# Which engine issues the rope's half-swaps: SyncE or ScalarE

## The chip, the cores and the metric

One core of a Trainium2 chip. The time is that of one execution of the whole program on the device, in microseconds (us): 3450.16 us, the median of 3 runs (3445.27 to 3460.52).

## The reference, cut to what matters

A sequence of 512 tokens of width 1024 goes through two blocks. The first has two layers (SwiGLU, stick-breaking attention or a linear recurrence, SwiGLU). The second has two *hybrid* layers, and the change lies in these alone:

```python
proj = h @ w_in                       # a_q, a_k, ..., b_q, ..., i_q, i_k, ..., c_q, c_k, ...
ya = moba_attention(apply_rope(heads(a_q, 6)), apply_rope(heads(a_k, 6)), heads(a_v, 6))
yb = dsa_attention(apply_rope(heads(b_q, 6)), rope1(b_k), b_v, apply_rope(heads(i_q, 4)), rope1(i_k), i_w)
yc = dilated_mixture(apply_rope(heads(c_q, 12)), apply_rope(heads(c_k, 12)), heads(c_v, 12))

def apply_rope(x, cos, sin):          # heads of 64 columns
    x1, x2 = x[..., :32], x[..., 32:]
    return concatenate([x1 * c - x2 * s, x1 * s + x2 * c])
```

Every rope needs, beside each half of 32 columns of a head, the other half. `dsa_attention` first scores all keys with the small index heads (i_q, i_k) and keeps the best; its selection precedes the heads B.

## The kernel before, in words

Activations lie transposed: columns of a projection on the partitions, the 512 tokens along the free axis. A projection is made in *panels* of 256 columns. For each panel SyncE loads 1 MB of weights into one of four `raw` buffers (L2523); ScalarE casts them to a high part (`w_high`, L1172); VectorE subtracts to get a low part (`w_low`, L1670); TensorE (PE) multiplies high by high, high by low and low by high into a pair of PSUM banks (L579). Each engine has its own program, written out in the order in which it shall work, and waits on semaphores for named steps. `take(key)` in an engine's program means: do the loads, casts or subtractions up to some panels ahead of this one. SyncE loads up to three panels ahead, ScalarE and VectorE one ahead.

A hybrid stage (`h0`, `h1`) has, before the heads, the panels i_q, a_v, i_k, a_q (two), a_k, a_v, a_g. Behind the first a_q panel stand the four index scores on PE (L914), whose sums VectorE makes and then searches for the largest (L2104, L2106). Then come 24 heads (6 A, 6 B, 12 C in three groups of four), pipelined: in step `i` PE turns the weights of head `i-2`, makes one panel that `L.fills` names for this step, makes the scores of head `i+1`, and the values of head `i-2`. ScalarE's order in step `i` is: copy of the turned weights (L1498), the exponentials of head `i-1` (L1504), `fill_rest`, `fill` (casts, then the copy out of PSUM), and `finish` of head `i-2` (L1243, or L1559 and L1566 for C). VectorE's is: row maximum of head `i` (L2154), weights of head `i-1` (L2167, L2170), the rope of the panel before, `w_low`, `finish`.

The rope of a panel, 13 of them in a stage:

1. ScalarE copies the product from PSUM to `rope_x` (`rope_copy`, L1441; step `roped_in`). It first waits until the previous rope has left `rope_x` (`x_free`).
2. The halves are swapped from `rope_x` into `rope_y` by DMA: four transfers of 32 partitions, 128 KB each (two of 64 KB for i_k). In the kernel before, SyncE does this (`swap`, L2579 to L2588): it waits for the copy and until the previous rope has left `rope_y` (`y_free`: its last `roped`), and issues the transfers. They stand in SyncE's program between the `take`s that load weights.
3. When they have landed (`swapped`), GpSimd multiplies the first half-panel by cos (L2410), VectorE the second (L2062), both by sin (L2063), and VectorE adds (L2066; step `roped`).

There is one `rope_x` and one `rope_y`. The ropes come in the order i_q, i_k, a_q 0, a_q 256, a_k 128, b_q 0, b_q 256, and for each C group c_q and c_k; from b_q on they are the fills of steps 0, 1, 5, 6, 9, 12, 15 and 16. Two more transfers on SyncE, `copy_half` (L2593), double the roped ik and bk.

Of the kernel before, what the change touches and what calls it, by code (L numbers as in the profile page):

```python
# [55 lines left out]
def build(nc, t, out):  # L56
# [6 lines left out]
    HD = 64  # L63
# [11 lines left out]
    with ExitStack() as ctx:  # L75
# [3 lines left out]
        def sem(name):  # L79
            return ctx.enter_context(nc.semaphore(name))  # L80
# [26 lines left out]
        with nc.sbuf_tensor("before_parts", [P, 12 * S], F32), nc.sbuf_tensor("sb_parts", [P, 4, TRI], F32R) as sb_parts:  # L107
# [15 lines left out]
        s_in, s_tab, s_swap, s_out, s_gate_w, s_dup = (sem(n) for n in (  # L123
            "x_loaded", "tables_loaded", "swapped", "stored", "gate_w_loaded", "copied_half"))
# [4 lines left out]
        def at(*step):  # L129

            return steps.get(step, (None, 0)) if counting[0] else steps[step]

        def fence(q, name):

            for engine in ENGINES:
                q.wait_ge(*at("past", name, engine))
# [152 lines left out]
        for m, (kind, i) in enumerate(entries):  # L289
# [4 lines left out]
            r = min(allowed, key=lambda r: -1 if newest_in[r] is None else newest_in[r])  # L294
# [865 lines left out]
        def scalar(q):  # L1160
            e = q.engine
# [15 lines left out]
            def taken_product(key):  # L1177
                q.wait_ge(*at("product", *key))
                b = base_of.get(key, 0)
                return psum[:, b:b + 2, :]  # L1180
# [251 lines left out]
            def hybrid(layer):  # L1432
                stage = f"h{layer}"
                L = hybrid_views(layer)

                def rope_copy(name, c0):

                    for step in L.x_free(name, c0):
                        q.wait_ge(*at(*step))
                    parts, n = L.parts(name, c0), len(L.dests[name, c0])  # L1440
                    e.copy(L.rope_x[0:parts[0], 0:n, :], taken_product((stage, name, c0))[0:parts[0], 0:n, :]).then_inc(  # L1441
                        *q.up(s_taken, "roped_in", stage, name, c0))

                def gate_sigmoid(name, c0):
                    dst = L.gates[name, c0]
                    n = dst.shape[1]
                    e.activation(dst, taken_product((stage, name, c0))[:, 0:n, :], ACT.Sigmoid).then_inc(*q.up(s_taken, "gate_sigmoid", stage, name, c0))
                    e.preload_act_table_set("natural_log_exp_and_others")
# [8 lines left out]
                q.mark("past", (stage, "area"), "ACT")  # L1457
                fence(q, (stage, "area"))
                rope_copy("i_q", 0)
                key = (stage, "a_v", 0)  # L1460
                q.wait_ge(*at("product", *key))
                b = base_of.get(key, 0)
                e.copy(L.av[:, :, 0:256], flat[:, b * 512:(b + 2) * 512].rearrange("p (t c) -> p t c", c=PANEL)).then_inc(*q.up(s_taken, "av", stage, 0))
                take((stage, "i_k", 0))
                rope_copy("i_k", 0)
                e.mul(L.SS[0][64:68, 0:S], psum[64:68, base_of.get((stage, "i_k", 0), 0), :], 1.0 / 16.0).then_inc(*q.up(s_taken, "iw_scaled", stage))
                take((stage, "a_q", 0))
                rope_copy("a_q", 0)
                q.wait_ge(*at("iw_turned", stage))
                e.copy(L.iw, psum[:, 5, 0:16].rearrange("p (n h) -> p n h", n=NT)).then_inc(*q.up(s_taken, "iw", stage))  # L1470
# [16 lines left out]
                b = base_of.get(("av_turned", stage), 0)  # L1487
# [128 lines left out]
            for j in range(KD):  # L1616
                q.wait_ge(*at("x_turned", j))
                b = base_of.get(("x_turned", j // 2 * 2), 0)
# [16 lines left out]
            rglru()  # L1635
            ffn("f3")
            hybrid(0)
            hybrid(1)
            spread("end2", 1)
            for n in range(NT):  # L1640
                q.wait_ge(*at("out_turned", n))
                b = base_of.get(("out", n), 0)
# [865 lines left out]
        def sync(q):  # L2508
            e = q.engine
# [23 lines left out]
            def take(key):  # L2533
                split_to(ahead_of(number[key]))

            def first_products(stage):
                split_to(number[stage, *FIRST[stage][0]] + 1)

            def project_back(stage, row0, last=True):
                if last:  # L2540
                    split_to(beyond_back(stage, row0, NC + 1))
                    return
                for c in range(NC):
                    take((stage, "back", row0, c))
# [30 lines left out]
            def hybrid(layer):  # L2575
                stage = f"h{layer}"
                L = hybrid_views(layer)

                def swap(name, c0):  # L2579

                    parts, n = L.parts(name, c0), len(L.dests[name, c0])
                    q.wait_ge(*at("roped_in", stage, name, c0))
                    for step in L.y_free(name, c0):
                        q.wait_ge(*at(*step))
                    for r in range(0, parts[0], HD):
                        m = sum(1 for p in parts[:n] if p > r)
                        for a, b in ((r, r + 32), (r + 32, r)):
                            e.dma_start(L.rope_y[a:a + 32, 0:m, :], L.rope_x[b:b + 32, 0:m, :]).then_inc(*q.up(s_swap, "swapped", stage, name, c0, by=16))  # L2588

                def copy_half(which, dst, *after):  # L2590
                    for step in after:
                        q.wait_ge(*at(*step))
                    e.dma_start(dst[HD:P, :, :], dst[0:HD, :, :]).then_inc(*q.up(s_dup, "copied_half", stage, which, by=16))  # L2593

                first_products(stage)
                fence(q, (stage, "area"))
                swap("i_q", 0)
                take((stage, "i_k", 0))
                swap("i_k", 0)
                take((stage, "a_q", 0))  # L2600
                copy_half("ik", L.ik, ("roped", stage, "i_k", 0, 0))
                swap("a_q", 0)
                take((stage, "a_q", 256))
                swap("a_q", 256)
                take((stage, "a_k", 128))
                swap("a_k", 128)
                take((stage, "a_v", 256))
                take((stage, "a_g", 128))
                for i in range(len(L.heads) + 2):
                    if i - 1 in L.fills and L.fills[i - 1][1:] == ("b_q", 256):  # L2610
                        copy_half("bk", L.bk, ("roped", stage, "b_q", 256, 0), ("roped", stage, "b_q", 256, 1))
                    if i in L.fills:
                        what, name, c0 = L.fills[i]
                        take((stage, name, c0))
                        if what == "rope":
                            swap(name, c0)
                take((stage, "m_g", 2 * D))
                for jj in range(KD // 2):
                    if jj:
                        for b in range(3):  # L2620
                            take((stage, "m_g", b * D + jj * PANEL))
                    take((stage, "branches", jj))
                project_back(stage, 0)


            for g, names in enumerate(groups):
                r = 0
# [20 lines left out]
            rglru()  # L2648
            ffn("f3")
            hybrid(0)  # L2650
            hybrid(1)
            for n in range(NT):
                q.wait_ge(*at("out_rows", n))
# [66 lines left out]
```

## Time and profile before

| of the profiled execution | |
|---|---|
| its own time | 3461.18 us |
| its span | 3459.5 us |
| PE busy | 3248.6 us, 94% |
| VectorE (DVE) busy | 1778.1 us, 51% |
| ScalarE (ACT) busy | 1171.5 us, 34% |
| GpSimd (POOL) busy | 165.8 us, 5% |
| mean granted clock of TensorE | 0.959 |
| chain that ended last | PE 81%, DVE 10%, ACT 5% |
| SyncE's swap transfers | 92 of 128 KB and 8 of 64 KB |

Engines work beside each other, so the busy times don't add up. The chain that ended last is followed back from the last instruction, at each step to what released it; it says which engine's work set the end. A row of the timeline has a start, a duration, engine, line and operation, and in square brackets how long the engine stood idle before it and what released it. DMA-issuing instructions aren't counted as busy; they stand on the issuing engine's queue, SPq for SyncE.

### The profile page before, as it was taken

How to read it: one execution, taken by the hardware profiler on the slowest of the kernel's cores; microseconds unless marked ns; L12 is line 12 of the kernel's file. 1: busy time of each engine (PE TensorE's matmuls, PEld its weight loads, DVE VectorE, ACT ScalarE, POOL GpSimd, SP SyncE). 2: the span in 40 equal slices, each digit the busy share in tenths (PEclk: the TensorE clock that was granted, in tenths of full speed). 3: DMA queues.
4: the chain of work that ended last, by engine and by line, in shares of the span. 5: the costliest groups of instructions: out<-in, count | busy, mean ns of one | idle time of the engine just before them, and what ended most of it. 6: DMA issues, size and time to landing. Idle time of an engine off the chain costs nothing.

```text
span 3459.5 us, 38825 instructions
## 1 busy us (share of the span) xinstructions
PE 3248.6 (94%) x16388; PEld 2685.2 (78%) x16388; DVE 1778.1 (51%) x2510; ACT 1171.5 (34%) x1523; POOL 165.8 (5%) x228
## 2 busy tenths in 40 slices
PE   3999998999999999999999998989989998999998
PEld 3887886788888888887888887656768876667687
DVE  5455543245555543357633335876543468655434
ACT  3212244543122322237432233233432323335322
POOL 0000011110000000002100000000000010000000
PEclk7999999999999999999999998999989998889898
DMA  4455521114555342231322223221212232212131
GB/s 178 158 195 170 172 84 49 49 62 158 195 177 176 123 157 97 92 111 54 101 98 98 98 74 92 78 67 57 74 50 96 77 113 67 60 50 74 61 98 49
DMA packets 286551, 353.72 MB, mean 102 GB/s; under 512 B 9458, under 2 KB 263210, under 8 KB 286378
## 3 DMA queue, kind: packets, MB, share of 16 engines
q1 hardware_dynamic: 286378, 351.23, 31.4%
q8 instruction: 130, 2.13, 0.3%
q14 instruction: 43, 0.35, 0.0%
HBM read 336.00 MB, written 2.10 MB: 98 GB/s over the span
## 4 chain that ended last, share of the span: by engine, by line
PE 81%; DVE 10%; ACT 5%; issue 1%; DMA 1%; POOL 1%; SPq 0%; DVEq 0%; ACTq 0%; POOLq 0%
PE psum L579 56%; PE psum L700 6%; PE psum L1104 3%; PE psum L658 2%; PE psum L600 2%; PE psum L973 2%; PE psum L1011 2%; DVE w_low L1670 1%; PE psum L776 1%; PE psum L989 1%; DVE psum L1798 1%; PE psum L545 1%; DVE h_low L1810 1%; DVE area L2106 1%; PE psum L654 1%
## 5 line engine op out<-in xcount | busy, mean ns | idle before, releaser
L579 PE MATMUL psum<-h_high,w_high 128*128 128x512 f32 (+1 forms) x2496 | 993.0, 398 | 51.7 <-DVE w_low L1670 22.0
L579 PE MATMUL psum<-h_low,w_high 128*128 128x512 f32 (+1 forms) x2496 | 984.3, 394 | 0.0
L579 PE MATMUL psum<-h_high,w_low 128*128 128x512 f32 (+1 forms) x2496 | 983.0, 394 | 0.0
L1670 DVE TENSOR_TENSOR w_low<-raw,w_high 128x2048 fp32r<-128x2048 f32 (+2 forms) x246 | 546.2, 2228 | 312.0 <-ACT w_high L1172 311.8
L1172 ACT CAST w_high<-raw 128x2048 fp32r<-128x2048 f32 (+3 forms) x254 | 464.2, 1840 | 546.5 <-DMA raw<-in_ffn_w_gu 253.2
L579 PEld LDWEIGHTS psum<-h_high,w_high 128*128 128x128 f32 (+1 forms) x2496 | 475.4, 190 | 163.1 <-issue 35.8
L579 PEld LDWEIGHTS psum<-h_high,w_low 128*128 128x128 f32 (+1 forms) x2496 | 475.2, 190 | 101.7
L579 PEld LDWEIGHTS psum<-h_low,w_high 128*128 128x128 f32 (+1 forms) x2496 | 475.9, 191 | 99.3 <-issue 1.0
L579 PE MATMUL psum<-y_high,w_high 128*128 128x512 f32 x592 | 233.8, 395 | 11.2 <-DVE w_low L1670 8.6
L1914 DVE TENSOR_TENSOR area<-area,psum 128x512 f32<-128x512 f32 x88 | 60.2, 684 | 342.1 <-PE psum L579 333.8
L579 PE MATMUL psum<-y_high,w_low 128*128 128x512 f32 x592 | 231.9, 392 | 0.0
L579 PE MATMUL psum<-y_low,w_high 128*128 128x512 f32 x592 | 231.8, 391 | 0.0
L1243 ACT CAST y_high<-area 128x512 fp32r<-128x512 f32 x102 | 62.7, 620 | 440.4 <-DVE area L1914 399.0
L1687 DVE SCALAR_TENSOR_TENSOR mod_acc<-raw,vec,mod_acc 128x1024 f32<-128x1024 f32 x126 | 161.9, 1285 | 72.6 <-DMA raw<-in_mod_w 66.8
L1842 DVE SCALAR_TENSOR_TENSOR xT<-psum,gain_out,xT 128x512 f32<-128x512 f32 (+1 forms) x156 | 90.8, 623 | 197.4 <-PE psum L579 158.0
L658 PE MATMUL psum<-h_high,w_high 128*128 128x256 f32 x448 | 134.7, 301 | 14.0 <-DVE w_low L1670 10.7
L579 PEld LDWEIGHTS psum<-y_high,w_high 128*128 128x128 f32 x592 | 111.9, 189 | 36.7 <-issue 10.5
L700 PE MATMUL psum<-y_high,w_high 128*128 128x256 f32 x480 | 139.1, 290 | 1.3 <-DVE w_low L1670 1.1
L700 PE MATMUL psum<-y_high,w_low 128*128 128x256 f32 x480 | 137.2, 286 | 0.0
L700 PE MATMUL psum<-y_low,w_high 128*128 128x256 f32 x480 | 137.2, 286 | 0.0
L658 PE MATMUL psum<-h_low,w_high 128*128 128x256 f32 x448 | 130.2, 291 | 0.0
L579 PEld LDWEIGHTS psum<-y_low,w_high 128*128 128x128 f32 x592 | 112.1, 189 | 23.3 <-issue 0.2
(279 smaller groups left out, 4419.2 us busy)
## 6 DMA issues: line engine op xcount, KB each, us to landing
raw<-in_ffn_w_gu SPq DMA_DIRECT2D x88, 1024.0 KB, 6.3
raw<-in_mod_w SPq DMA_DIRECT2D x72, 1024.0 KB, 5.1
raw<-in_w_in SPq DMA_DIRECT2D x64, 1024.0 KB, 5.2
raw<-in_ffn_w_down SPq DMA_DIRECT2D x32, 1024.0 KB, 7.5
raw<-in_ffn_w_down SPq DMA_DIRECT2D x16, 768.0 KB, 4.8
raw<-in_sb_w_qkv SPq DMA_DIRECT2D x12, 1024.0 KB, 5.1
area<-area SPq DMA_DIRECT2D x92, 128.0 KB, 2.4
raw<-in_lru_w_in SPq DMA_DIRECT2D x10, 1024.0 KB, 5.3
```

The lines of the kernel that those rows point to most:

```text
L579: mm = e.matmul(psum[0:width, base + m, :], wv[a][:, at_k, c0:c0 + width], X[b][:, k, :], start=(at_k == 0 and (a, b) == (0, 0)), stop=(at ...
L600: mm = e.matmul(flat[:, o:o + n], X[b][:, k, tt * P:(tt + 1) * P], wv[a][:, k, :], start=(k == 0 and (a, b) == (0, 0)), stop=(k == KD - 1 ...
L658: mm = e.matmul(psum[:, base + m, HALF[h]], wv[a][:, k, m * P:(m + 1) * P], H[b][:, k, HALF[h]], start=first, stop=last)
L700: mm = e.matmul(psum[:, bank, m * S // 2:(m + 1) * S // 2], wv[a][:, at_k, m * P:(m + 1) * P], X[b][:, k, HALF[h]], start=(at_k == 0 and ( ...
L973: m = e.matmul(flat[:, ROW_AT[n]:ROW_AT[n] + P * (n + 1)], L.q_of(kind, ti)[r0:r0 + HD, n * P:(n + 1) * P], L.k_of(kind, h)[:, 0:P * (n + ...
L1011: m = e.matmul(psum[r0:r0 + HD, OUT, kt * P:S], L.v_of(kind, h, kt), L.PT[:, COL_AT[kt]:COL_AT[kt] + S - P * kt], start=kt == 0, stop=kt = ...
L1104: mm = e.matmul(psum[:, base + m, :], wv[x][:, k, m * P:(m + 1) * P], Y[y][:, k, :], start=(k == k0 and (x, y) == (0, 0)), stop=(k == k1 - ...
L1172: e.copy(w_high[x % NW][:, :n], raw[raw_at[m]][:, :n]).then_inc(*q.up(s_high, "w_high", x))
L1243: e.copy(Y[0][:, k, :], src).then_inc(*q.up(s_act, "y_high", stage, j))
L1670: e.tensor_tensor(w_low[raw_at[m]][:, :n], raw[raw_at[m]][:, :n], w_high[x % NW][:, :n].bitcast(F32), ALU.subtract).then_inc(*q.up(s_low, ...
L1687: g = e.scalar_tensor_tensor(mod_acc[:, :], w, c, mod_acc[:, :], ALU.mult, ALU.add)
L1842: return e.scalar_tensor_tensor(dst, src, gain_out[:, j:j + 1], dst, ALU.mult, ALU.add)
```

## The change

The swaps move from SyncE's program into ScalarE's, behind the copy in `rope_copy`. ScalarE waits for the previous rope to leave `rope_y`, then for its own copy, and issues the same two or four transfers; it goes on with its own program behind them. The transfers, their semaphore and all that waits for them stay. SyncE's program keeps the loads and `copy_half`, in the same order.

```diff
@@ rope_copy (ScalarE) @@
                     e.copy(L.rope_x[0:parts[0], 0:n, :], taken_product((stage, name, c0))[0:parts[0], 0:n, :]).then_inc(
                         *q.up(s_taken, "roped_in", stage, name, c0))
+                    for step in L.y_free(name, c0):
+                        q.wait_ge(*at(*step))
+                    q.wait_ge(*at("roped_in", stage, name, c0))
+                    for r in range(0, parts[0], HD):
+                        m = sum(1 for p in parts[:n] if p > r)
+                        for a, b in ((r, r + 32), (r + 32, r)):
+                            e.dma_start(L.rope_y[a:a + 32, 0:m, :], L.rope_x[b:b + 32, 0:m, :]).then_inc(*q.up(s_swap, "swapped", stage, name, c0, by=16))
@@ hybrid (SyncE) @@
-                def swap(name, c0):
-
-                    parts, n = L.parts(name, c0), len(L.dests[name, c0])
-                    q.wait_ge(*at("roped_in", stage, name, c0))
-                    for step in L.y_free(name, c0):
-                        q.wait_ge(*at(*step))
-                    for r in range(0, parts[0], HD):
-                        m = sum(1 for p in parts[:n] if p > r)
-                        for a, b in ((r, r + 32), (r + 32, r)):
-                            e.dma_start(L.rope_y[a:a + 32, 0:m, :], L.rope_x[b:b + 32, 0:m, :]).then_inc(*q.up(s_swap, "swapped", stage, name, c0, by=16))
...
-                swap("i_q", 0)
                 take((stage, "i_k", 0))
-                swap("i_k", 0)
                 take((stage, "a_q", 0))
                 copy_half("ik", L.ik, ("roped", stage, "i_k", 0, 0))
-                swap("a_q", 0)
                 take((stage, "a_q", 256))
-                swap("a_q", 256)
                 take((stage, "a_k", 128))
-                swap("a_k", 128)
...
                     if i in L.fills:
                         what, name, c0 = L.fills[i]
                         take((stage, name, c0))
-                        if what == "rope":
-                            swap(name, c0)
```

## Rows read from the trace of the kernel before

**Rows 1.** Line L2588: count, duration min/median/max in ns; last row its landings.

```profile
L2588 SPq DMA_DIRECT2D area<-area x100: 507/591/672, 2130.0 to 3138.6; - x100
...
DMA to landing us min/median/max: 2.0/2.4/4.3
```

**Rows 2.** Waits of SyncE's queue, whole span: us in total, times, longest.

```profile
SPq L2588 <- ACT area L1441: 262.7, 20, 26.1
```

**Rows 3.** Line L1172 (casts), 2120 to 2545 us: count, durations; idle before it.

```profile
L1172 ACT CAST w_high<-raw x22: 1055/1898/1912, 2123.2 to 2522.8; 128x2048 fp32r<-128x2048 f32 x21, 128x1024 fp32r<-128x1024 f32 x1
...
  PE psum L658: 1.8, 1
```

**Rows 4.** Timeline of SyncE's queue, stage h0: start us, duration us, issues.

```profile
2132.60 1.34 SPq L2523 DMA_DIRECT2D raw<-in_w_in  x2
2139.11 1.15 SPq L2588 DMA_DIRECT2D area<-area  x2
...
2173.26 2.41 SPq L2588 DMA_DIRECT2D area<-area  x4
...
2245.25 2.41 SPq L2588 DMA_DIRECT2D area<-area  x4
...
2410.14 2.64 SPq L2588 DMA_DIRECT2D area<-area  x4
...
2463.47 2.41 SPq L2588 DMA_DIRECT2D area<-area  x4
```

**Rows 5.** Timeline of VectorE, stage h0.

```profile
2138.33 0.69 DVE L2066 TENSOR_TENSOR y_plain<-y_plain,area 128x512 f32<-128x512 f32 x1
...
2177.47 0.69 DVE L2063 TENSOR_TENSOR area<-area,rope_s 128x512 f32<-128x512 f32 x1 [3.60 <-DMA area<-area]
...
2466.08 0.69 DVE L2154 SCALAR_TENSOR_TENSOR area<-psum,inv 128x512 f32<-128x512 f32 x1 [2.33 <-PE psum L989]
```

**Rows 6.** Chain that ended last, 2128 to 2150 us: start us, us, what.

```profile
2138.47 0.59 ACT area L1466
...
2139.09 1.92 ACT w_high L1172
...
2141.03 2.29 DVE w_low L1670
2143.32 1.70 DVE area L2063
...
2148.10 2.27 PE psum L914 x9
```

**Rows 7.** Timeline of GpSimd at i_k, stage h0.

```profile
2143.10 1.36 POOL L2410 TENSOR_TENSOR y_plain<-area,rope_c 64x512 f32<-64x512 f32 x1 [6.80 <-DMA area<-area]
```

**Rows 8.** Landings of L2588 at 2137 to 2145 us (i_k), at 2845 to 2855 us (a_k).

```profile
DMA to landing us min/median/max: 2.3/2.8/3.3
...
DMA to landing us min/median/max: 2.3/2.4/4.3
```

**Rows 9.** Timeline of ScalarE behind three of its copies, stage h0.

```profile
2247.72 1.01 ACT L1498 COPY area<-psum 128x1024 f32<-128x1024 f32 x1 [2.50 <-PE psum L989]
...
2414.32 1.02 ACT L1498 COPY area<-psum 128x1024 f32<-128x1024 f32 x1 [4.21 <-PE psum L989]
...
2463.34 0.21 ACT L1559 ACTIVATE mod_acc<-mod_acc 128x4 f32<-128x4 f32 x1
```

**Rows 10.** Waits of PE, 2120 to 2545 us: us in total, times, longest.

```profile
PE psum L973 <- DVE y_plain L2073: 5.9, 1, 5.9
...
PE psum L579 <- ACT area L1540: 3.2, 1, 3.2
...
PE psum L914 <- DMA y_plain<-y_plain: 2.4, 1, 2.4
```

**Rows 11.** Chain that ended last: the first two products among the heads of h0.

```profile
2217.87 12.75 PE psum L579 x48
...
2232.97 11.12 PE psum L579 x48
```

## The prediction

> **What bounds the kernel now.** I read the page first. TensorE is busy for 94% of the span and the chain that ended last is 81% PE, so an edit is worth only what it does to PE's waits. The table by line then finds the thing that changes: 100 swap transfers, 50 in each of the two hybrid stages, a median of 0.591 us each for the issue and 2.4 us from issue to landing, all on SyncE's queue [rows 1]. Next come the waits, asked from both ends. What did the swaps keep SyncE from doing? It stood 262.7 us at the head of swap groups waiting for ScalarE's copy [rows 2], with weight loads queued behind. Did a load then come late? The weight casts of the first hybrid stage show one idle stretch, 1.8 us, and its releaser is PE, not a DMA [rows 3]; the second stage answers the same. So SyncE has no time to give back. Last I followed the chain and the timelines around each of the 13 groups of a stage, asking of each: what does ScalarE do in the 2.4 us behind its copy, and who waits for that?
>
> **The change part by part.** The sum is made against the profiled execution, 3461.2 us (span 3459.5); the median of the runs shown is 3450.2, and I carry the difference over to it.
>
> *Taken from SyncE.* 100 × 0.59 = 59 us of issuing and the waits ahead of it. Worth nothing, by the casts that wait for no load [rows 3].
>
> *Given to ScalarE.* Per group one wait for its own copy, one for the previous rope, and four issues (two for i_k). No row shows an issue on ScalarE. The nearest is the same transfer on SyncE: four take 2.41 us, two take 1.15 [rows 4], and I take that, 0.6 us each. Below lies nothing at all (a sequencer that hands the work on and runs ahead); above I set 1.2 us, twice SyncE's median [rows 1]. 0.6 is the only measured price of this very transfer, and both ends are kept as rivals. A wait for its own semaphore I cost at under 0.1 us.
>
> *i_k: on the chain.* Its swaps must wait until the rope of i_q is done, 2138.33 + 0.69 = 2139.02 [rows 5]. Today SyncE does that waiting, and ScalarE goes on with L1466 at 2138.47 and the next weight cast at 2139.09 [rows 6]. Afterwards ScalarE waits itself: swaps from 2139.1 to 2140.3, L1466 to 2140.9, the cast 1.8 us later than now. Everything behind it hangs on that cast in the chain of waits: VectorE's w_low at 2141.03, the rope's multiply L2063, the copy of half of ik by DMA, and PE's index scores at 2148.10, which wait 2.4 us for that copy [rows 6, 10]. A little comes back. L2063 takes 1.70 us here [rows 6] against 0.69 where it runs alone [rows 5], because GpSimd's multiply runs beside it from 2143.10 to 2144.46 [rows 7]; when VectorE comes later, GpSimd is partly done. Between 0 and 1.0 back, I take 0.6: **+1.2 us**.
>
> *i_q and a_q 256: the swaps meet a load.* Today SyncE issues the next loads only after the swaps, at 2132.60 [rows 4]. Freed, it issues them when their buffer is released, about when ScalarE starts its copy, so each group of swaps travels beside 1 MB or 2 MB of weights. VectorE sits 3.60 us waiting for the swaps of a_q 256 [rows 5], and the rope of i_q starts the i_k chain above, so these two landings count. A swap of i_k that now travels beside two loads landed in 3.3 us, and the longest of all took 4.3 [rows 8], against 2.4. From 0 to 1.9 each; I take 0.4, since the group's last swap starts 1.8 us behind its first, when the load is mostly through: **+0.8 us** for the two.
>
> *b_q 256: just covered.* The issues would end at 2245.25 + 2.41 = 2247.66 [rows 4], and ScalarE's next work, L1498, waits for PE until 2247.72 [rows 9]. Behind it stands L1540, for which PE waits 3.2 us [rows 10]: there is no reserve left, and every 0.1 us that an issue costs above 0.6 is 0.4 us of PE. **+0.1 us.**
>
> *c_k 512: the last one.* ScalarE's issues run from 2463.47 to 2465.88, and L1559 (0.21 us, at 2463.34 today) comes behind them, to 2466.1 [rows 4, 9]. VectorE's finish of head 14 waits for L1559, and behind that in VectorE's order stands the row maximum L2154, today at 2466.08 [rows 5], on which PE's next scores wait. **+0.3 us.**
>
> *The other nine cost nothing*, each by a named cover. At c_q 0, c_k 0, c_q 256 and c_k 256 ScalarE's next instruction waits for PE or VectorE until after the issues would end; the tightest is c_k 256, 2410.14 + 2.64 = 2412.8 against 2414.32 [rows 4, 9]. At a_k, b_q 0 and c_q 512 a cast or exponentials come up to 2.4 us later, and a product of 48 matmuls, 11.12 us [rows 11], lies before PE asks for their results. At i_q the copy of a_v moves behind the issues, and its banks are wanted much later. At a_q 0 a small copy (L1470) waits; PE wants it only at the second index head, which the i_k term has itself pushed back. If these covers go, the price is what an issue costs above 0.6, times four.
>
> A longer gap of PE ahead of the index scores could lower the clock behind it. The first product after the 5.9 us gap at the heads' start took 12.75 us against 11.12 for the next of its kind [rows 10, 11]; the gap here grows only from 2.4 to about 4, so 0 to 1.6 us a stage, in the range and not in the sum.
>
> Sum per stage 1.2 + 0.8 + 0.1 + 0.3 = 2.4 us, twice: **+4.8 us**, 3466.0 for such an execution and **3455 us** on the median.
>
> **The rivals.**
> *ScalarE hardly pays (3452).* If an issue costs it nothing, i_k still waits for the rope (cast 0.6 us later, half of it recovered) and the collisions stay: 0.3 + 0.8 = 1.1 a stage, +2.2. For it: nothing but that SyncE's number need not be ScalarE's. Against: SyncE's four issues stand back to back, 2.41 us, as long as a landing [rows 1, 4]. The Trainium skill's page "DMA: Bandwidth & Descriptors", section "Issuing engines are not separate DMA queues", says that issuing from several engines saves only the sequencer's time to start a DMA and calls that usually small beside the DMA; by that rule this rival holds. The rows here disagree on the size.
>
> *The swaps are slowed (3463).* Every landing on the chain goes from 2.4 to 4.3 us [rows 8]: i_q and a_q 256 cost 1.9 each, and at c_k 512 GpSimd's rope comes 1.9 later, of which about 1.0 reaches VectorE. 1.2 + 3.8 + 0.1 + 1.3 = 6.4 a stage, +12.8. For it: the loads now always start beside the swaps. Against: today's median of 2.4 lies near the least landing, 2.0 [rows 1], and a queue of its own takes a swap from behind the load. The same page, section "Queues, rings and completion order", has each DMA engine take turns between queues by packet, so a swap beside a load would get a share at once; that would keep this term small, and no row of one queue can show it.
>
> *An issue costs ScalarE 1.2 us (3470, slower).* Then i_k: 2139.02 + 2.4 + 0.59 − 2139.09 = 2.9; a_q 0: L1470 behind 4.8 us of issues makes the second index head about 1.4 late; b_q 256: 2245.25 + 4.8 − 2247.72 = 2.3, straight into PE's wait for L1540; c_k 512: 2463.47 + 4.8 + 0.2 − 2466.08 = 2.4; collisions 0.8. Together 9.8 a stage, +19.6. It turns slower by more than this kernel's measurement can tell (0.5%, 17 us) from about 1.1 us an issue on. For it: ScalarE's queue also carries compute. Against: only that SyncE does it in 0.59.
>
> *Freed loads make it faster (below 3433).* For it: the 262.7 us of SyncE's waiting [rows 2]. Against: no cast waits for a load [rows 3], and the only returns in sight are the 1.0 us at L2063 and a few tenths of landing.
>
> **How the numbers follow.** The forecast 0.55, ScalarE hardly pays 0.17, swaps slowed 0.10, issue at 1.2 us 0.14, faster 0.04. The first three lie within 0.5%, 0.82; part of the swaps-slowed case could add to the forecast's other terms, so 0.02 of it goes to slower: same 0.80, slower 0.16, faster 0.04. The range: the median itself was seen between 3445 and 3461; below, the first rival less a few us of that, 3446; above, the 1.2 us case, 3470, and 3 more for the clock: 3473.
>
> **What would show it.** In the changed trace the 100 issues stand on ScalarE's queue with a mean near 0.6 us, and a second hardware queue carries the swaps' packets. The load at 2132.60 starts some 3.5 us earlier against the product; the swaps of i_q and a_q 256 land in under 3 us. The first cast behind i_k comes 1.8 us later, and PE's gap ahead of the index scores grows from 2.4 us to between 3 and 4.3 in both stages. PE's wait for L1540 stays at 3.2 us. The prediction is wrong if an issue on ScalarE takes over 1 us (PE's wait for L1540 shows it first), if ScalarE's instructions behind the swaps don't move at all, or if casts are found that start earlier relative to PE than before.

## The result and the profile after

The changed kernel takes **3473.56 us**, the median of 5 runs (3465.08 to 3484.05), against 3450.16: a ratio of 1.0071 [1.0050, 1.0092], 23 us slower. A second measurement of it gave 1.0053 [1.0041, 1.0065]. The profiled execution took 3473.56 us with a span of 3471.8, 12.3 us more than the span before; the mean granted clock is 0.959 in both. So the profiles show 12.3 us, and 7 to 11 us of the medians' difference must be sought elsewhere.

First the moved instructions in the table by line (count, shortest, median and longest issue in ns; then the landings), and the packets by queue on the page.

```profile
L1449 ACTq DMA_DIRECT2D area<-area x100: 514/613/877, 2128.8 to 3150.5; - x100
...
DMA to landing us min/median/max: 2.0/5.0/7.3
```

```profile
q1 hardware_dynamic: 281578, 338.64, 29.8%
q10 hardware_dynamic: 4800, 12.59, 1.4%
```

The swaps stand on ScalarE's queue at 0.613 us each and travel in a hardware queue of their own, both as forecast. What was not: from issue to landing they take 5.0 us at the median, where SyncE's took 2.4 [rows 1].

Next the landings of three groups of h0, asked by stretch: i_q (issued from 2128.8), a_q 256 (from 2176.1), and b_q 256 (from 2250.8).

```profile
DMA to landing us min/median/max: 6.3/6.6/6.8
...
DMA to landing us min/median/max: 4.7/4.9/5.0
...
DMA to landing us min/median/max: 2.1/2.2/2.4
```

What travels beside them stands on SyncE's queue, which before was held back to 2132.60 [rows 4].

```profile
2127.77 5.91 SPq L2530 DMA_DIRECT2D raw<-in_w_in  x3
```

Two weight loads of 1 MB are issued in a row as the copy of i_q starts, at 2127.77 and 2128.18, and a third at 2133.31, before its swaps have landed; these take 6.6 us beside them. SyncE's queue shows no load from 2215 to 2260 but one at 2236.11: the swaps of b_q 0, issued from 2237.2 on, land in 5.0 us, those of b_q 256 in 2.2. The queue of their own is as fast as the old one when nothing else moves.

The chain that ended last, from the copy of i_q to the index scores (start us, us, what):

```profile
2127.78 1.02 ACT area L1441
...
2130.76 6.78 DMA area<-area
...
2137.70 1.81 POOL y_plain L2417
...
2142.26 0.51 ACTq L1449
2142.78 0.31 issue
2143.09 2.13 DMA area<-area
...
2150.10 2.30 DMA y_plain<-y_plain
2152.40 0.14 issue
2152.54 3.70 PE psum L914 x10
```

Before, this chain went through ScalarE's cast and VectorE's w_low, with no swap in it [rows 6]. Now the landing of i_q's swaps is a link of it. The chain as printed also goes through i_k's swaps, at 2143.09, but the timelines of ScalarE, VectorE and GpSimd around i_k, with idle time in brackets, show that nothing waited for these in the end:

```profile
2142.26 1.34 ACTq L1449 DMA_DIRECT2D area<-area  x2
2143.65 0.59 ACT L1473 ACTIVATE area<-psum 4x512 f32<-4x512 f32 x1 [2.00 <-issue]
2144.26 1.90 ACT L1172 CAST w_high<-raw 128x2048 fp32r<-128x2048 f32 x1
...
2146.19 2.57 DVE L1677 TENSOR_TENSOR w_low<-raw,w_high 128x2048 fp32r<-128x2048 f32 x1 [3.96 <-ACT w_high L1172]
2148.69 0.67 DVE L2070 TENSOR_TENSOR area<-area,rope_s 64x512 f32<-64x512 f32 x1
...
2145.35 1.26 POOL L2417 TENSOR_TENSOR y_plain<-area,rope_c 64x512 f32<-64x512 f32 x1 [5.84 <-DMA area<-area]
```

GpSimd is done with i_k at 2146.61, while VectorE's w_low, which waited for ScalarE's cast, runs to 2148.76, and the rope's multiply follows it at once. The rope of i_q ends at 2142.23; two issues and L1473 lie between that and the cast, which began 0.07 us behind the rope before [rows 5, 6] and now begins 2.0 behind it. What PE waits for, 2110 to 2260 us (total, times, longest), and VectorE's wait at a_q 256:

```profile
PE psum L914 <- DMA y_plain<-y_plain: 7.8, 1, 7.8
PE psum L973 <- DVE y_plain L2080: 5.0, 1, 5.0
PE psum L579 <- DVE w_low L1677: 4.1, 1, 4.1
PE psum L579 <- ACT area L1547: 3.2, 1, 3.2
```

```profile
2182.86 0.69 DVE L2070 TENSOR_TENSOR area<-area,rope_s 128x512 f32<-128x512 f32 x1 [4.95 <-DMA area<-area]
```

The gap ahead of the index scores went from 2.4 to 7.8 us [rows 10]. VectorE's wait for the swaps of a_q 256 went from 3.60 to 4.95 [rows 5]; behind it stands the subtraction for the a_v panel, and PE's gap ahead of that product went from 1.4 to 4.1. L1547, the old L1540, holds PE for 3.2 us as before [rows 10]. Stage h1 answers alike, with gaps of 7.6 and 4.4.

**The other part: the clock among the heads.** A stage's 24 heads mostly last about 329 or about 338 us. The difference lies in one stretch, 160 to 240 us behind the first head's scores. Here are its rows in h0 and h1 (stretch, length, busy us and instructions of each engine, granted clock, DMA share, GB/s), before and then after:

```profile
2373.30:2453.30 80.00, 73.53 (x374) 54.75 (x373) 46.76 (x86) 32.65 (x75) 3.80 (x5) 0.98 0.22 61
3036.80:3116.80 80.00, 73.52 (x328) 53.02 (x327) 45.01 (x82) 29.09 (x66) 3.67 (x4) 0.87 0.19 53
```

```profile
2378.70:2458.70 80.00, 74.06 (x377) 55.20 (x376) 47.14 (x86) 32.45 (x75) 3.69 (x4) 0.98 0.25 71
3050.60:3130.60 80.00, 74.06 (x329) 53.26 (x329) 45.70 (x82) 29.09 (x66) 3.74 (x4) 0.87 0.19 53
```

PE is as busy in all four. At 0.98 it is nearly always at 2.4 GHz; at 0.87 it spends about a quarter of the stretch at 1.2 GHz and does some 46 matmuls less. That is 0.11 of 80, an estimate of **8.8 us**, called a spell below. PE's waits don't tell the two apart. Here are those of the kernel before in its h0 stretch, at 0.98; the one of h1, at 0.87, answers with the same two lines:

```profile
PE psum L966 <- DVE area L2154: 3.3, 2, 1.9
PE psum L973 <- DVE area L2154: 3.2, 1, 3.2
```

Both profiles hold one spell, so their 12.3 us are free of it. The single runs are not: the five of the changed kernel stand at 3465.1 with a mean clock of 0.962, 3473.4 and 3473.6 at 0.958 and 0.959, and 3482.5 and 3484.1 at 0.956 and 0.955, steps of about one spell. The kernel before has a mean clock of 0.9625 over 86 runs, and its profile, with one spell, lies 9 us above the median of these runs, 3451.9. By this reading the changed kernel has about one spell more.

### The profile page after: what moved, and what is told of

It is laid out like the page before. It is cut to its first block, busy times and chain, and to the rows that moved or that the text cites. A ratio compares the mean times of both kernels' runs of the same rounds, so it can differ in the third digit from the quotient of the medians.

```text
span 3471.8 us, 38819 instructions
## 1 busy us (share of the span) xinstructions
PE 3250.6 (94%) x16388; PEld 2684.7 (77%) x16388; DVE 1774.5 (51%) x2510; ACT 1172.5 (34%) x1523; POOL 171.0 (5%) x228
## 4 chain that ended last, share of the span: by engine, by line
PE 79%; DVE 11%; ACT 5%; DMA 2%; issue 1%; POOL 1%; ACTq 1%; SPq 0%; DVEq 0%; POOLq 0%
PE psum L579 55%; PE psum L700 6%; PE psum L1104 3%; PE psum L658 2%; PE psum L600 2%; PE psum L1011 2%; PE psum L973 2%; DVE w_low L1677 2%; PE psum L776 1%; PE psum L989 1%; DVE psum L1805 1%; DMA area<-area 1%; PE psum L545 1%; DVE area L2113 1%; DVE h_low L1817 1%
## 5 line engine op out<-in xcount | busy, mean ns | idle before, releaser
L1172 ACT CAST w_high<-raw 128x2048 fp32r<-128x2048 f32 (+3 forms) x254 | 464.3, 1840 | 558.0 <-DMA raw<-in_ffn_w_gu 255.3
```

Source lines behind the costliest of these rows:

```text
L1172: e.copy(w_high[x % NW][:, :n], raw[raw_at[m]][:, :n]).then_inc(*q.up(s_high, "w_high", x))
```

## The experiments

"Before" stands for the kernel before, run on the same chip. *Ahead* is what each profile needs from the end of the i_q product to the heads, both stages together, less the 169.1 us of before; *heads* is the length of the two stages of heads. Both are worked out from PE's timeline.

| run | median, us | over before | mean clock | ahead, us | heads, us |
|---|---|---|---|---|---|
| before | 3450.2 to 3453.5 | | 0.9625 | 0 | 330, 340 |
| changed | 3473.6 | +23.4 | 0.958 | +16.6 | 329, 337 |
| a0 changed again | 3472.7 | +19.2 | 0.9584 | +12.9 | 336, 328 |
| e1 held at all | 3461.1 | +7.6 | 0.9617 | +4.5 | 330, 339 |
| e2 loads first, SyncE | 3473.1 | +19.6 | 0.9578 | +14.8 | 332, 328 |
| e4 held, i_k by SyncE | 3453.7 | +0.2 | 0.9629 | +2.4 | 330, 330 |
| b4 held at i_q | 3467.0 | +16.1 | 0.9592 | +7.4 | 332, 328 |
| c1 held at a_q 256 | 3466.4 | +14.2 | 0.9608 | +12.1 | 331, 329 |
| c2 held at both | 3469.1 | +16.9 | 0.9592 | +8.1 | 337, 336 |
| e3 heads only, by ScalarE | 3448.6 | −2.4 | 0.9631 | −1.6 | 329, 339 |
| c3 the same again | 3451.3 | −1.0 | 0.9618 | −1.5 | 329, 338 |
| c4 before, a_v's w_low late | 3470.4 | +18.1 | 0.9590 | +2.3 | 338, 339 |
| d4 before, PE waits | 3469.3 | +19.0 | 0.9575 | +1.1 | 339, 340 |
| d1 c4 and idle products | 3455.5 | +5.1 | 0.9625 | −3.3 | 332, 336 |
| b1 changed, idle at scores | 3470.1 | +19.1 | 0.9620 | +9.8 | 336, 329 |
| b2 before, idle in two gaps | 3452.6 | +1.6 | 0.9637 | −6.7 | 335, 335 |
| d2 changed, idle at a_v | 3469.4 | +19.0 | 0.9617 | +17.2 | 329, 329 |
| d3 changed, idle at both | 3470.6 | +20.3 | 0.9619 | +11.6 | 337, 329 |

**The changed kernel once more.**

> The changed kernel once more, beside the kernel before on the same chip. The two profiled executions differ by 12.3 us at the same mean clock (0.959), the medians by 23.4. If the change costs only its waits, the ratio is near 1.0036 (12 us); if it also costs clock, or if the first medians were no accident, near 1.007 (23 us).

3472.71 us, ratio 1.0053 [1.0041, 1.0065]; the landings have a median of 5.0 us again.

**Is it the loads beside the swaps?** First ScalarE keeps the swaps, and SyncE waits at each of their old places until they have landed:

```diff
+                def held(name, c0):
+                    q.wait_ge(*at("swapped", stage, name, c0))
+                held("i_q", 0)
                 take((stage, "i_k", 0))
...
+                            held(name, c0)      # behind each rope's take among the heads
```

> ScalarE issues all swaps as in the changed kernel, but SyncE waits, at the places where it used to issue them, until they have landed, and loads only then. Theory 1 (the loss is the landing of swaps that now travel beside weight loads): landings back to a median of 2.4 us (5.0 in the changed kernel), PE's gap ahead of the index scores from 7.8 to about 4.2 us, and 3 to 6 us over the kernel before in all. Theory 2 (the loss is ScalarE's: its waits, its issue time of 0.61 us each, or a slow queue of its own): the landings or the gap stay as in the changed kernel, 12 us or more over the kernel before.

3461.13 us, ratio 1.0021 [1.0012, 1.0031]. The opposite edit leaves ScalarE alone: SyncE issues the swaps as before, but each time the next load ahead of them.

```diff
+                take((stage, "i_k", 0))
                 swap("i_q", 0)
-                take((stage, "i_k", 0))
+                take((stage, "a_q", 0))
                 swap("i_k", 0)
```

> The kernel before, all swaps on SyncE, but each next weight load is issued ahead of the swaps in place of behind them; ScalarE is untouched. Theory 1: landings rise from 2.4 to 5 us or more, as the swaps now share the DMA engines with the loads or stand behind them in one queue, and the time rises by 6 to 14 us. Theory 2: as the kernel before, within 2 us.

3473.11 us, ratio 1.0061 [1.0044, 1.0077]: the whole loss, with nothing given to ScalarE. The transfer lists of the page (transfer, queue, count, size, median us to landing) are those of the two kernels, e1 first:

```profile
area<-area ACTq DMA_DIRECT2D x92, 128.0 KB, 2.4
```

```profile
area<-area SPq DMA_DIRECT2D x92, 128.0 KB, 5.1
```

and the gaps ahead of the index scores, again e1 first, go with them (7.8 in the changed kernel):

```profile
PE psum L914 <- DMA y_plain<-y_plain: 4.5, 1, 4.5
```

```profile
PE psum L914 <- DMA y_plain<-y_plain: 8.4, 1, 8.4
```

So for the landing it doesn't matter who issues, nor in which queue: 5.0 us beside a load in a queue of its own, 5.1 behind it in one queue, 2.4 with the load held back. The wait that SyncE used to make for ScalarE's copy [rows 2] kept the loads away from the swaps, and that was its use.

**The issues on ScalarE's path at i_k.** As e1, with i_k's two swaps issued by SyncE, on a semaphore of their own:

```diff
+                    if (name, c0) in (("i_k", 0),):
+                        return                  # ScalarE, behind its copy
+                    if (name, c0) in (("i_k", 0),):    # SyncE, in held
+                        for a, b in ((r, r + 32), (r + 32, r)):
+                            e.dma_start(L.rope_y[a:a + 32, 0:m, :], L.rope_x[b:b + 32, 0:m, :]).then_inc(
+                                *q.up(s_swap2, "swapped", stage, name, c0, by=16))
```

> As the kernel with held loads, but the two swaps of i_k stay on SyncE (a semaphore of their own), so that ScalarE doesn't wait there for the rope of i_q ahead of its next cast. My sum gave this term 1.2 us a stage after the overlap with GpSimd, 1.8 before it: theory 1 expects 2 to 4 us less than with all on ScalarE, so 0 to 3 us over the kernel before, and PE's gap ahead of the index scores back near 2.4 us. Theory 2 expects the same step down, but from 12 us or more.

3453.68 us, ratio 1.0005 [0.9994, 1.0017], 7.5 us below e1. The traces give 2.1 us of that ahead of the heads, in size what the i_k term of two stages allows, but they don't show it to be that term: in h0 the index scores come only 0.1 us sooner behind the i_q product than in e1, since the cast at i_k now waits 2.0 us for a weight load that was held back, and in h1 1.2 us sooner. And e4's heads have no spell in the profile and e1's have one.

**The two collisions one by one**, by holding SyncE only there. At i_q (`held("i_q", 0)` alone):

> The changed kernel, with SyncE held at one place only: after i_q, until its swaps have landed. Theory 1 says that the two loads beside the swaps of i_q (6.6 us to landing, 2.4 before) are the largest single part: PE's gap ahead of the index scores falls from 7.8 to about 4 us in both stages, so at least 7 us of the loss come back, and with the clock in step 10; 6 to 10 us over the kernel before stay. If the collisions of a_q 256 or of the heads carried the loss, the time stays 15 us or more above.

3467.03 us, ratio 1.0042 [1.0029, 1.0056]: 3.4 and 3.8 us less to the index scores in the two stages, and the gap ahead of a_v at 5.5 us in h0. At a_q 256 alone:

> The changed kernel with one wait more: in SyncE's program, at the old place of the swaps of a_q 256, it waits until these have landed before it loads the next panel. The collision at i_q stays. All theories: the swaps of a_q 256 land in about 2.4 us again, VectorE's wait for them falls from 4.95 to about 3 us, and PE's gap ahead of the a_v product from 4.1 to about 1.4 us; the gap ahead of the index scores stays at 7.6. Theory T4 (what brings the slow spells of the clock among the heads is the longer gap ahead of the a_v product): mean clock back to about 0.962, median 3460, before +8 to +11. Rival A (each late landing costs its own gap and no more): 2.5 us a stage come back, before +14 to +17. Rival B (it is the gap ahead of the index scores): clock stays at 0.958 and the median at 3468 or more.

3466.44 us, ratio 1.0040 [1.0024, 1.0056]. The edit did half of what was expected: the gap ahead of a_v fell to 1.5 us, but a second of 2.4 us opened ahead of the next product. The profile shows no spell in either stage, yet the median is +14, so this clean pair of stages proves nothing for the other runs. At both places:

> The changed kernel with SyncE held at two places of a stage, until the swaps of i_q and until those of a_q 256 have landed; the other eleven groups, i_k and the heads among them, travel beside loads as in the changed kernel. If the collisions at these two places are the whole of the loss beside ScalarE's issues: like the kernel that holds SyncE at all thirteen (before +7.5), so +4 to +9, with a mean clock of 0.962. If landings of 5 us at the other groups cost something too: +12 or more.

3469.08 us, ratio 1.0042 [1.0027, 1.0058], against +4 to +9. The index scores come 2.1 us later than before in each stage, as in e1, but the a_q 256 part came back only in part and both stages of heads have their spell. Whether the landings of the other eleven groups cost something of their own or the spells are all of it was not separated.

**ScalarE's swaps among the heads only.** The five early ropes stay with SyncE; ScalarE issues the eight among the heads, and SyncE's loads run free there.

```diff
+                    if (name, c0) in (("i_q", 0), ("i_k", 0), ("a_q", 0), ("a_q", 256), ("a_k", 128)):
+                        return                  # SyncE issues these
-                        if what == "rope":
-                            swap(name, c0)
```

> SyncE issues the five groups ahead of the heads, at its old places; ScalarE issues the eight among the heads, where SyncE runs ahead freely, so that those swaps collide with loads (5 us to landing). My covers say that neither ScalarE's issues nor the later landings reach PE there: within 2 us of the kernel before. If the slow spells of the clock among the heads come from the change, 8 us or more above it.

> The mixed version once more: SyncE issues the swaps of the five ropes ahead of the heads at their old places, ScalarE those of the eight ropes among the heads, where SyncE's loads run free. To see whether its ratio of 0.9989 [0.9977, 1.0000] is a gain. If it is: ratio 0.998 to 0.9995 again. If it was chance: 0.9995 to 1.001. It is not above 1.0015 in either case, since the landings of 5 us among the heads are covered by PE's products.

Ratios 0.9989 [0.9977, 1.0000] and 0.9996 [0.9985, 1.0007], 12 runs each: no loss, and no gain that can be told from none. The nine covers at which the forecast priced a later ScalarE at nothing, as far as they lie among the heads, hold, late landings included.

**Which gap brings the spells?** First the gap ahead of the index scores: 32 idle products of 128x512 fill it in the changed kernel; the kernel before gets idle products in its own two gaps ahead of the heads.

```diff
+                wait_free(0)
+                for _ in range(32):             # 10 in the kernel before, and 25 ahead of the heads
+                    e.matmul(psum[:, 0, :], H[0][:, 0, 0:P], H[0][:, 0, :], start=True, stop=True)
```

> The changed kernel with 32 idle products (128x512, a bank that is overwritten afterwards) on PE in its longer gap ahead of the index scores; nothing else moves. The two stages' waits explain some 12 us of the loss of 19 to 23; theory 3: the rest is clock that PE loses behind the longer gap. Then the idle products bring 5 to 10 us back, to 3462 to 3467. If the rest has another cause, the time stays near 3472.

> The kernel before with idle products in the two gaps that it has ahead of the heads: 10 ahead of the index scores (gap 2.4 us), 25 ahead of the first head (5.9 us). Theory 3: the first product among the heads takes 11.1 us in place of 12.8 and slow spells become fewer, 3 to 8 us below the kernel before. Else no change within 2 us.

3470.05 us, ratio 1.0046 [1.0025, 1.0067], and 3452.59, ratio 0.9998 [0.9986, 1.0010]. Their profiles reach the heads sooner (+9.8 us against +16.6 and +12.9 of the changed kernel, and −6.7 against 0), and neither median shows it. The profile of b2 has a granted clock of 0.87 in both stretches, so filling these gaps didn't keep the spells away. Then the gap ahead of a_v, in the kernel before: VectorE makes that panel's w_low three search steps later.

```diff
+                some(3)
                 take((stage, "a_k", 128))
-                some(5)
+                some(2)
```

> The kernel before, all swaps with SyncE, with one change in VectorE's order: the subtractions that make w_low for a_v are moved behind three more steps of the search for the largest scores, so that they end some 3 us later and PE's gap ahead of the a_v product grows from 1.4 to about 4 to 5 us in both stages; VectorE's sum of work and all transfers stay. Theory T4 (a longer gap at this place brings slow spells of the clock among the heads): mean clock 0.958 to 0.960, median +10 to +14 over before. Rival A (a gap costs its own length): +6. Rival C (the stage has slack behind it, VectorE being ahead by the time the heads begin): 0 to +3, clock 0.962.

3470.35 us, ratio 1.0050 [1.0036, 1.0064], more than any theory gave, although the trace has only 2.3 us of it ahead of the heads. The edit makes two things late, PE and VectorE; two kernels part them. d1 fills the gap with idle products; d4 has VectorE's old order, and PE alone waits for a step of it.

```diff
+                if key[1:] == ("a_v", 256):      # d1, on c4
+                    for _ in range(20):
+                        e.matmul(psum[:, base, :], H[0][:, 0, 0:P], H[0][:, 0, :], start=True, stop=True)
...
+                q.wait_ge(*at("held_av", stage)) # d4, on the kernel before: VectorE's second search step
                 b = columns("a_v", 256)
```

> The kernel before with the subtractions for a_v three search steps later, as in the version that gave +18 us, and in addition 20 idle products of 128x512 on TensorE ahead of the a_v product (some 4.5 us into a bank that the product then overwrites), so that the gap of 4.8 us is filled. Theory G (a gap of PE at this place brings the spells of lower clock among the heads): no spells, the two stages of heads at about 329 us, mean clock 0.962 or more, before +3 to +6. Theory V (VectorE's lateness at the heads' start does): still two spells of 338 us, before +15 to +18.

> The kernel before with VectorE's order kept and one more wait of PE: ahead of the a_v product it waits for the second step of VectorE's search behind the subtractions for a_v, so that its gap there grows from 1.4 to some 4 us, while VectorE runs as before. Theory G: spells in both stages, before +10 to +18, clock 0.959. Theory V: no more spells than before; the later product is taken up by the 5.9 us that PE waits for VectorE at the heads' start, before +0 to +3, clock 0.962.

d1: 3455.46 us, ratio 1.0008 [0.9998, 1.0018]. d4: 3469.32 us, ratio 1.0046 [1.0029, 1.0062]. Here are d4's waits ahead of the heads, and then its two stretches of heads:

```profile
PE psum L579 <- DVE area L2107: 3.8, 1, 3.8
PE psum L974 <- DVE y_plain L2074: 3.5, 1, 3.5
PE psum L914 <- DMA y_plain<-y_plain: 2.4, 1, 2.4
```

```profile
2373.30:2453.30 80.00, 73.51 (x328) 53.02 (x327) 44.94 (x82) 29.10 (x66) 3.69 (x4) 0.87 0.19 53
3045.80:3125.80 80.00, 73.52 (x329) 52.95 (x328) 45.02 (x82) 29.10 (x66) 3.68 (x4) 0.87 0.19 53
```

PE's wait for the heads' first operands shrank from 5.9 to 3.5 us and took the later product up, so that 1.1 us is left ahead of the heads; a spell in both stages, some 18 us against a median run of before with none, fits the rest of the 19 us. In the kernel before, then, a gap of 4 us at this one place, some 190 us ahead of the stretch, goes with a spell in both stages, and with idle products in the gap 13 of c4's 18 us are gone; 5.6 of these stand ahead of the heads in the profiles, and d1's stretches are at 0.94 and 0.89. How the gap acts so far behind isn't shown. The waits of PE inside the stretch are the same with and without a spell, so a rival is that it matters when these waits come: any edit ahead that shifts them in time could then bring a spell or take it away, whatever gap it fills. No run separates the two, and b2 fits the rival better.

**The same in the changed kernel**, with 17 idle products ahead of a_v, and with these and the 32 ahead of the scores:

> The changed kernel with 17 idle products (some 3.9 us) in its gap of 4.1 us ahead of the a_v product; all else as changed. Theory G: clock back to 0.962, median 3460 to 3463 (the direct part, +8 to +11, stays). Theory V or mere chance: clock 0.9585, 3469 to 3474.

> The changed kernel with idle products in both longer gaps, 32 ahead of the index scores and 17 ahead of the a_v product. Theory G: as with the second alone, 3460 to 3463. Theory G2 (either gap is enough to bring spells, which is why filling the first alone moved it only to 3470): only this kernel comes to 3460 to 3463, the one with the second alone stays near 3470. Theory V: 3467 or more here too.

3469.38 us, ratio 1.0047 [1.0031, 1.0063], and 3470.63, ratio 1.0052 [1.0033, 1.0072]: nothing came back that can be told from none, although the a_v gap was down to 0.6 us in d2 and neither of its profiled stages has a spell. That profile, at 3467.9 us, lies near d2's median; its way to the heads is the longest of all, +17.2 us. So what is shown for the kernel before isn't shown for the changed one. What decides there when a spell comes stays open.

## Why the prediction was wrong, step by step

Forecast 3455, range 3446 to 3473, "same" 0.80; measured 3473.6, just above the range and slower by 0.71%. The direction was right, and the issue price, i_k and b_q 256 came as priced.

- **Taken from SyncE: nothing gained.** Right that no cast was waiting, wrong that this ends it. The freed SyncE issues its loads with the start of i_q's copy (2127.77 and 2127.78), where they began 3.65 us behind it before (2132.60 and 2128.95): the 3.5 us that were forecast. These loads slowed what was on the path.
- **Issue price on ScalarE.** Forecast 0.6 us, measured 0.613. The rivals "ScalarE hardly pays" and "an issue costs 1.2 us" both fall. The Trainium skill's page "DMA: Bandwidth & Descriptors", section "Issuing engines are not separate DMA queues", states that DMAs of all issuing engines interleave on the same DMA engines and that only initiation time is saved. The trace agrees as far as the landings go, 5.0 us in a queue of its own against 5.1 behind the loads in one; I had weighed only the half about the price.
- **i_k: +1.2 a stage.** In h0 the time from the end of i_q's rope to the index scores went from 2148.10 − 2139.02 = 9.08 to 2152.54 − 2142.23 = 10.31, +1.23. Right, and by the way that was forecast: the cast comes 1.96 us later behind the rope (1.8 forecast), 1.03 come back at L2070 (0.67 us against 1.70), which now runs behind GpSimd's multiply, and w_low beside that multiply gives up 0.28 (2.57 against 2.29).
- **"i_q and a_q 256: the swaps meet a load", +0.8: the step that failed.** I saw the collision and took 0.4 us each from a range of 0 to 1.9, on the ground that the load is mostly through when the group's last swap starts, 1.8 us behind its first. It was not: a load of 1 MB takes 5.3 us at the median, SyncE issues two in a row at i_q and one at a_q 256 (2174.87), and the swaps landed 4.2 and 2.5 us later than before, in 6.6 and 4.9 where the forecast's own sign was under 3. The trace of before already had the time of such loads: the five from 2125 to 2180 us landed in 5.3 us at the least, the second of two in a row in 9.3. At i_q, by the timelines of h0, the time from the copy's end to the rope's start went from 4.54 to 8.91 us: +4.4 a stage, straight to the index scores. At a_q 256 the late swaps made the a_v product 2.7 us later in h0, of which 0.9 was taken up by a shorter gap at the heads' start. That is some 5 to 6 us in h0 where the sum had 0.8 a stage: 4.4 + 1.8 by these waits, 6.6 − 1.2 by the whole way to the heads. The upper bound, 4.3 us, was the worst landing of a kernel in which loads were held back [rows 8]; a row of before can't bound a collision that before avoided. The rival "the swaps are slowed" named the mechanism and was undersized too. The Trainium skill's page "DMA: Bandwidth & Descriptors", section "Queues, rings and completion order", has each DMA engine take turns between queues by packet, and the forecast took from it that this term stays small. That doesn't follow here, with 6.6 us beside the loads; whether the engines take turns so, no run shows.
- **b_q 256 and the covers.** PE's wait for L1547 is 3.2 us, as forecast. With e3 at no loss, the terms of the heads, c_k 512 among them, are too small to be measured.
- **The clock.** I allowed 0 to 1.6 us a stage, right behind the index scores. In h1's profile more than that came there (below). More came as spells of 8.8 us far behind, which the forecast didn't have at all; about 7 to 11 us of the medians' difference goes with them. What brings them in the changed kernel is open.

By profiles: to the index scores +5.6 and +5.7 us, from there to the heads +1.0 and +4.3, the heads −0.8 and −2.5, the stretches outside −0.9, together 12.3. The +5.6 are the 4.4 of i_q and the 1.2 of i_k. The 4.3 of h1 is more than h0's 1.0 by a lower clock in the same 229 matmuls (0.87 against 0.92 before, PE busy 4.2 us longer), not by a longer wait; the second profile of the changed kernel has +0.5 there.

## What to carry to other kernels

A wait that costs its own engine nothing may be what keeps two transfers apart: before moving it, ask which transfers will then start beside the one that is waited for, and bound the landing by a transfer that had such company. A queue of its own did not shield a small transfer. Where the profile has stretches of different clock, a small edit far ahead can go with more time there than in its own wait (d4: 1.1 us ahead of the heads, 19 in all), so compare the profiled stretches and the medians apart.

## What the runs showed that was not expected

- A swap of 128 KB inside the chip's memory lands in 2.2 to 2.4 us alone and in 5.0 us at the median of the changed kernel (5.1 behind the loads in one queue, e2); beside the two loads at i_q it took 6.6 us in a queue of its own and 7.3 behind them (e2). With a queue of their own the swaps slow the load as well: the second of the two loads landed in 12.0 us, against 9.3 before and 8.6 in e2, where the swaps stand behind it.
- With a longer gap of PE at one place (1.4 to 3.8 us, d4) the granted clock was lower some 190 us later, 0.87 in place of 0.98 over 80 us in h0, while PE's busy time in that stretch stayed at 73.5 us. The h1 of before has the same 0.87 without the longer gap.
